# The second block's mixer reordered: memory units first, small work behind units, all 31 convolution taps on DVE

## The reference

```python
h = rms_norm(x, norm_mix_g[l]);  p = h @ w_in[l]
y_a = conformer_conv(p[:256], p[256:512], ...)   # h = a * sigmoid(g); 31-tap causal depthwise conv; layer norm; silu
y_b = head_rms_norm(moba_attention(q, k, v))      # 4 heads of 64; with 256 tokens it is one causal block
q_c, k_c, v_c = ...                               # 4 heads, 64 keys, 128 values
log_a = log_sigmoid(p_gate @ gla_gate_w + b) / 16
y_c = head_rms_norm(gla_chunked(q_c, k_c, v_c, log_a)) * silu(r)   # chunks of 32, a state of 64x128 handed on by chunk
x = x + concat([y_a, y_b, y_c]) @ w_out[l]
h = rms_norm(x, norm_ffn_g[l]);  x = x + (silu(conv3(h @ up_a)) * conv3(h @ up_g)) @ w_down
```

## Time and profile before

| | us |
|---|---|
| median of 3 runs | 2491.24 (2490.52 to 2492.51) |
| the profiled execution | 2489.02 |
| its span | 2487.2 |
| PE / DVE / ACT / POOL busy | 2311.9 / 1768.5 / 1313.8 / 194.9 |
| mean granted clock of PE | 0.944 |

### The profile page before, as it was taken

How to read it: one execution, slowest core, us unless ns; L and a number is a source line. 1 busy time by engine, 2 the same in 40 slices (tenths; PEclk the granted TensorE clock), 3 DMA queues, 4 the chain that set the end, 5 groups by cost and what they waited for, 6 DMA issues and landing times.

```text
span 2487.2 us, 42276 instructions
## 1 busy us (share of the span) xinstructions
PE 2311.9 (93%) x16453; PEld 2158.5 (87%) x16453; DVE 1768.5 (71%) x1847; ACT 1313.8 (53%) x1230; POOL 194.9 (8%) x174
## 2 busy tenths in 40 slices
PE   7998998999699999999999999996878998978998
PEld 7898997999599999999999999995858997867997
DVE  4466445456488889898888888886846776745777
ACT  4543433454277777676767776763413443422443
POOL 1000000000000000000000000003900001930000
PEclk9999998999699999999999999998859998958999
DMA  9344554535299999999999999994404545412541
GB/s 294 103 152 139 200 187 154 167 110 163 70 360 344 357 341 355 340 354 340 354 346 352 343 353 343 354 360 135 136 0 141 188 170 163 134 40 92 188 169 67
DMA packets 429633, 556.97 MB, mean 224 GB/s; under 512 B 9719, under 2 KB 385253, under 8 KB 429521
## 3 DMA queue, kind: packets, MB, share of 16 engines
q1 hardware_dynamic: 425376, 544.85, 64.8%
q0 software_dynamic: 4144, 10.64, 1.5%
HBM read 554.39 MB, written 1.06 MB: 223 GB/s over the span
## 4 chain that ended last, share of the span: by engine, by line
issue 45%; PE 40%; POOL 4%; DVE 3%; POOLq 2%; ACT 2%; DVEq 2%; DMA 1%; SPq 0%; ACTq 0%
PE ps L612 11%; PE ps L613 11%; PE ps L614 11%; POOLq L592 2%; POOL st L593 2%; POOL st L587 2%; PE ps L1220 1%; ACT w_hi L1272 1%; PE ps L1200 1%; DMA w<-in_w_in 1%; PE ps L1217 0%; PE ps L801 0%; DMA raw<-in_w_in 0%; PE ps L652 0%; DVE xn L1724 0%
## 5 line engine op out<-in xcount | busy, mean ns | idle before, releaser
L1639 DVE TENSOR_TENSOR w_lo<-raw,w_hi 128x2048 fp32r<-128x2048 f32 x519 | 1185.2, 2293 | 350.4 <-ACT w_hi L1272 347.9
L1272 ACT ACTIVATE w_hi<-raw 128x2048 fp32r<-128x2048 f32 x519 | 987.4, 1908 | 252.9 <-PE ps L614 241.8
L612 PE MATMUL ps<-w_hi,xg_hi 128*128 128x256 f32 x1792 | 512.2, 286 | 11.0 <-DVE xg_lo L2026 8.1
L612 PE MATMUL ps<-xT_hi,w_hi 128*128 128x256 f32 x1760 | 504.4, 287 | 16.2 <-DVE xT_lo L1654 8.3
L614 PE MATMUL ps<-w_hi,xg_lo 128*128 128x256 f32 x1792 | 500.6, 279 | 0.0
L613 PE MATMUL ps<-w_lo,xg_hi 128*128 128x256 f32 x1792 | 500.6, 279 | 0.0
L613 PE MATMUL ps<-xT_lo,w_hi 128*128 128x256 f32 x1760 | 499.5, 284 | 0.0
L614 PE MATMUL ps<-xT_hi,w_lo 128*128 128x256 f32 x1760 | 499.3, 284 | 0.0
L612 PEld LDWEIGHTS ps<-xT_hi,w_hi 128*128 128x128 f32 x1760 | 339.5, 193 | 23.0 <-DVE xT_lo L1654 9.1
L612 PEld LDWEIGHTS ps<-w_hi,xg_hi 128*128 128x128 f32 x1792 | 338.2, 189 | 17.7 <-issue 12.1
L613 PEld LDWEIGHTS ps<-w_lo,xg_hi 128*128 128x128 f32 x1792 | 340.2, 190 | 3.4
(11 more groups left out here) (448 smaller groups left out, 2954.3 us busy)
## 6 DMA issues: line engine op xcount, KB each, us to landing
raw<-in_exp_w SPq DMA_DIRECT2D x336, 1024.0 KB, 5.8
raw<-in_ffn_w_up SPq DMA_DIRECT2D x44, 1024.0 KB, 5.1
raw<-in_w_in SPq DMA_DIRECT2D x42, 1024.0 KB, 6.6
raw<-in_ffn_w SPq DMA_DIRECT2D x33, 1024.0 KB, 5.1
raw<-in_ffn_w_down SPq DMA_DIRECT2D x22, 1024.0 KB, 5.4
raw<-in_w_gate SPq DMA_DIRECT2D x16, 1024.0 KB, 5.3
raw<-in_w_out SPq DMA_DIRECT2D x8, 1024.0 KB, 4.9
raw<-in_w_o SPq DMA_DIRECT2D x6, 1024.0 KB, 6.1
```

The source lines that it names most:

```text
L612: pe.matmul(out, lhs[0], rhs[0], start=first, stop=False)
L1272: act.activation(w_hi[:, u.const % SPL, 0:width], raw[:, u.const % RAW, 0:width], ACT.Copy)\
L1639: dve.tensor_tensor(w_lo[:, u.const % SPL, 0:width], raw[:, u.const % RAW, 0:width], w_hi[:, u.const % SPL, 0:width].bitcast(F32), ALU.sub ...
```

## The change

The order of the units becomes: convolution (0, 1), q and k of the memory (2, 3), its values (4, 5), q, k, v of the attention (6 to 8), r (9, 10). Two PSUM banks take the projections instead of four, so a unit waits for the copy of the one two before. The small work is spread over the list of PE behind the units that give its inputs: the scores within chunks (`within_chunks`: 4 transposes and 8 matmuls) behind unit 5, all state steps behind unit 6 without waits between them, attention scores and the GLA output behind unit 7, the pairs of attention heads around and in unit 9 (`between` runs after its first half), the transposes of the results in the middle of units 10 and 11. The state steps use keys padded with zeros (`kdz`, 128 columns of which 64 are nonzero for each head, so that two heads give 128 partitions), the GLA output uses queries masked by chunk (`qgm`) and puts tokens on partitions, so its norm is a column of statistics (bn_stats) instead of matmuls with ones and a diagonal. POOL zeroes the two tiles and has no taps; DVE does all 31, in pieces of 6, 4, 3, 6, 5 and 7. The four w_out units are taken by rows (256 rows, 1024 columns) in the order 2, 1, 3, 0, so each needs a quarter of y: GLA heads 0 and 1, attention, GLA heads 2 and 3, convolution; each is 24 products of 512 columns, and the sums are closed in the last. x is then updated by quarters of 512 columns (`sums_to_x`, as after the feed-forward). The exponential subtracts the maximum by a bias on ACT instead of a pass on DVE, the gain of the attention's norm is a column of cols2, and attention and GLA outputs get their gains in the copies from PSUM. ACT's list follows the new order, with `ahead(n)` (the split of unit n+2) apart from `out(n, ...)` (wait for unit n, copy it). Before the first tap nothing moves.

The diff, cut to its core (removed lines of the old order are left out; lines with + are new, those with a blank stay):

```diff
-POOL_TAPS = range(0, 18)
-IN2_COLS = (0, 256, 512, 768, 1024, 1280, 1536, 1792, 2048, 2320, 2576)
+IN2_COLS = (0, 256, 1280, 1536, 1792, 2048, 512, 768, 1024, 2320, 2576)
+OUT2_ROWS = (2, 1, 3, 0)
+OUT2_BANKS = (1, 2, 4, 5)
...
+                pool.memset(kdz[:], 0.0)
+                pool.memset(qgm[:], 0.0).then_inc(S_.zeroed2, 1)
...
+                def state_steps():
+                    pe.wait_ge(S_.kd_ready, L + 1)
+                    pe.wait_ge(S_.at_ready, L + 1)
+                    for n in range(NCH - 1):
+                        rows = slice(GCH * (n % 4), GCH * (n % 4) + GCH)
+                        for c in range(2):
+                            for half in range(2):
+                                h = 2 * c + half
+                                m = pe.matmul(bank(4 + n % 4, 2, 2, GDV)[:, n // 4, c, :], kdz[rows, 2 * (n // 4) + c, half, :],
+                                              vc[rows, n // 4, h * GDV:(h + 1) * GDV], start=half == 0, stop=half == 1)
+                    m.then_inc(S_.ds_psum, 1)
+                def scores(tile, banks):
...
+                def gla_out():
+                    for h in range(GH):
+                        rows = slice(64 * (h % 2), 64 * (h % 2) + 64)
+                        for t in range(TT):
+                            o = ps[:, 5 + h % 2, (2 * (h // 2) + t) * P:(2 * (h // 2) + t + 1) * P]
+                            pe.matmul(o, atT[:, h, t, :], vc[:, t, h * GDV:(h + 1) * GDV], start=True, stop=False)
+                            for j in range(t == 0, 4):
+                                m = pe.matmul(o, qgm[rows, h // 2, t, j, :], st8[rows, 4 * t + j, h // 2, :],
+                                              start=False, stop=j == 3)
+                    m.then_inc(S_.o_psum, 1)
...
+                def w_out(n, chunks, between=None):
+                    pe.wait_ge(S_.yT2_lo_ready, L * 4 + n + 1)
+                    w = unit_parts(u + (11 + n), 2, D)
+                    for q, (t, h) in enumerate(QUARTERS):
+                        if between and q == 2:
+                            between()
+                        for c in range(2):
+                            m = product(ps[:, OUT2_BANKS[q], :], [v[:, t * P:(t + 1) * P] for v in chunks[c]],
+                                        [v[:, c, h * HALF:(h + 1) * HALF] for v in w], n == 0 and c == 0, n == 3 and c == 1)
+                        if n == 3 and q < 3:
+                            m.then_inc(S_.sums_closed, 1)
+                    m.then_inc(S_.unit_used, 1)
...
                 T(0, L * 8 + 24)
+                columns()
+                gate_rank()
                 T(2)
+                gate_logits()
                 T(3)
                 tok(4)
+                tok(5)
+                within_chunks()
                 T(6)
+                state_steps()
+                T(7)
+                pe.wait_ge(S_.state_ready, L + 1)
+                pe.wait_ge(S_.proj2_out, L * 11 + 8)
+                scores(0, (2, 3))
+                scores(1, (4, 7))
+                gla_out()
                 tok(8)
+                next_pair = attention(L, HB, (sb0, sb1), pT2, vb, (S_.pT2_psum, S_.pT2_ready, S_.pv2), (2, 3),
+                                      (ps[:, 4, 0:256], ps[:, 4, 256:512]))
+                pe.wait_ge(S_.proj2_out, L * 11 + 9)
...
+                pe.wait_ge(S_.proj2_out, L * 11 + 9)
+                pe.wait_ge(S_.expd2, L + 1)
+                next_pair(0)
+                tok(9, lambda: next_pair(1))
+                next_pair(2)
                 pe.wait_ge(S_.conv_ready, L + 1)
+                channel_sum(0, cvT, S_.csum_psum)
+                tok(10, lambda: gated_T(0))
+                def both_T():
+                    attended_T()
+                    pe.wait_ge(S_.yT2_lo_ready, L * 4 + 1)
+                    gated_T(1)
...
+                ahead(0)
+                ahead(1)
+                dve.wait_ge(S_.proj2_out, L * 11 + 2)
+                dve.tensor_tensor(avT[:, :, CW - 1:], avT[:, :, CW - 1:], agT[:], ALU.mult)
+                dve.drain()
+                dve.wait_ge(S_.p2_cols_ready, L + 1)
+                ahead(2)
+                convolve(6)
+                dve.wait_ge(S_.glog_psum, L + 1)
+                for c in range(2):
+                    m = dve.tensor_scalar(laT[:, c, :], ps[:, 7, c * S:(c + 1) * S], cols2[:, 68 + c:69 + c], None, ALU.add)
+                m.then_inc(S_.glog_in, 1)
+                ahead(3)
+                convolve(4)
...
+                ahead(4)
...
                 convolve(3)
...
+                dve.wait_ge(S_.gexp_ready, L * 2 + 1)
+                for c in range(2):
+                    m = dve.tensor_tensor(ends[:, c], spread(gam[:, c, :], 2, GCH), ends[:, c], ALU.subtract)
+                m.then_inc(S_.rest_ready, 1)
+                dve.wait_ge(S_.zeroed2, L + 1)
+                dve.wait_ge(S_.proj2_out, L * 11 + 4)
...
+                dve.tensor_tensor(laT[:], kcT[:], laT[:], ALU.mult)
+                dve.drain()
+                dve.tensor_tensor(qcT[:], qcT[:], egT[:], ALU.mult)
+                dve.wait_ge(S_.gexp_ready, L * 2 + 2)
+                dve.tensor_tensor(cumT[:], kcT[:], cumT[:], ALU.mult).then_inc(S_.qkg_ready, 1)
+                ahead(5)
+                convolve(6)
+                ahead(6)
+                dve.wait_ge(S_.at_psum, L + 1)
...
+                m.then_inc(S_.at_ready, 1)
+                convolve(5)
+                ahead(7)
+                dve.wait_ge(S_.ds_psum, L + 1)
...
+                        if n == 0:
+                            m = dve.tensor_copy(st8[:, 1, c, :], step)
+                        else:
+                            m = dve.scalar_tensor_tensor(st8[:, n + 1, c, :], st8[:, n, c, :], dec[:, c, n:n + 1], step,
+                                                         ALU.mult, ALU.add)
+                    if n < NCH - 2:
+                        dve.drain()
+                m.then_inc(S_.state_ready, 1)
...
+                negative_max(sb0[:], col(160, 4))
+                negative_max(sb1[:], col(164, 4))
+                ahead(8)
+                dve.wait_ge(S_.o_psum, L + 1)
+                o = [(t, h, ps[:, 5 + h % 2, (2 * (h // 2) + t) * P:(2 * (h // 2) + t + 1) * P]) for t in range(TT) for h in range(GH)]
+                var = moments([b for _, _, b in o])
+                dve.scalar_tensor_tensor(col(96, 8), var, RMS_EPS, col(104, 8), ALU.add, ALU.add).then_inc(S_.sqrt2_in, 1)
+                convolve(CW - taps[0])
+                dve.wait_ge(S_.expd2, L + 1)
+                for t, sc in enumerate((sb0, sb1)):
...
+                ahead(9)
+                dve.memset(stat[:, 0:1], 0.0).then_inc(S_.conv_ready, 1)
+                ahead(10)
...
+                gated(0)
                 dve.wait_ge(S_.pv2, L * HB + HB)
...
+                m.then_inc(S_.yb_ready, 1)
+                low(yM_lo[:, 0:2, :], 3, 70, yM_hi[:, 0:2, :], 1)
+                gated(1)
+                ahead(11)
+                low(yA_lo[:, 2:4, :], 0, 74, yA_hi[:, 2:4, :], 2)
+                low(yM_lo[:, 2:4, :], 3, 72, yM_hi[:, 2:4, :], 3)
...
+                ahead(12)
+                dve.wait_ge(S_.sqrt2_out, L * 5 + 4)
...
+                ahead(13)
+                ahead(14)
+                sums_to_x(u + 14, L * 6 + 3, None, half_square, OUT2_BANKS)
+                rms_norm(L * 5 + 5, L * 32 + 32, S_.xn_ready, 122, 2)
```

More of the change, by code:

```diff
@@ new lines, in within_chunks @@
+                def within_chunks():
+                    pe.wait_ge(S_.qkg_ready, L + 1)
+                    for t in range(TT):
+                        for c in range(2):
+                            m = pe.transpose(ps[:, 2, (2 * t + c) * P:(2 * t + c + 1) * P], kdT[:, c, t * P:(t + 1) * P], ident)
+                    m.then_inc(S_.kd_psum, 1)
+                    for h in range(GH):
+                        rows = slice(64 * (h % 2), 64 * (h % 2) + 64)
+                        for t in range(TT):
+                            m = pe.matmul(bank(3 + h % 2, 2, TT, P)[:, h // 2, t, :], kgT[rows, h // 2, t * P:(t + 1) * P],
+                                          qgT[rows, h // 2, t * P:(t + 1) * P], start=True, stop=True)
+                    m.then_inc(S_.at_psum, 1)
@@ new lines, in channel_sum @@
+                def channel_sum(col, src, done):
+                    for c in range(2):
+                        m = pe.matmul(ps[:, 7, col:col + S], ones, src[:, c, :], start=c == 0, stop=c == 1)
+                    m.then_inc(done, 1)
+                def w_out(n, chunks, between=None):
[3 more added lines that the diff above has]
+                        if between and q == 2:
+                            between()
+                        for c in range(2):
+                            m = product(ps[:, OUT2_BANKS[q], :], [v[:, t * P:(t + 1) * P] for v in chunks[c]],
[3 more added lines that the diff above has]
+                    m.then_inc(S_.unit_used, 1)
@@ L1179, in mixer2 @@
```

(45 more changed lines are left out.)

507 lines of the change are left out of this document (194 added, 313 removed).

## The result

| | before | after |
|---|---|---|
| median | 2490.88 (2490.22 to 2492.51) | 2450.19 (2449.38 to 2451.68) |
| the profiled execution | 2489.02 | 2449.39 |
| its span | 2487.2 | 2447.7 |
| mean granted clock of PE | 0.944 | 0.961 |

The ratio is 0.9836 (95% interval 0.9819 to 0.9853): 1.6% or 41 us less, clear of the noise, where 77 us were forecast, and outside the range of 2401 to 2443.

What follows compares the result with a forecast made beforehand. PE, busy 93%, was taken as the bound, losing time to waits and low clock in the second block's mixers. Saving 40.4 us less 2 for handoffs, 38.4 a layer, 77 for both: 2491.2 - 77 = 2414 us, range 2401 to 2443.

Steps and rivals of the forecast that it cites:

- (g): Mixer's tail: after the last w_lo, four quarters of 1.41 us on DVE, rms 0.9, xn at 1850.4.
- walk to xn: Layer 1's steps (a) to (g), summed without handoffs: xn at 1850.4 instead of 1890.8, 40.4 us earlier.
- (a): DVE's chain to qkg_ready ends at 1759.5, PE's units at 1755.0, so PE waits 4.5 us in within_chunks.
- rival 3: Taps keep 1.45 us instead of 0.96, their slowness not being POOL's: 13.3 us a layer, 2441; chance 0.09.
- (b): Clock falls in PE's 4.5 us gap: within_chunks takes 3.3 instead of 2.2, T(6) 5.76 + 2.9, to 1771.5.
- (c): DVE reaches at_ready at 1771.0; PE's state_steps take 6.3 us to 1777.8, T(7) runs to 1783.6.
- The tie: In (c): T(7)'s copy done at 1784.2, DVE's state steps beside it at 1784.1.
- (d): PE: scores 1.6, gla_out's 72 instructions 8.1, tok(8) 5.8, to 1799.9; DVE's conv_ready at 1808.4.
- (e): Attention pairs to first output product: conv_ready 1.9 to spare, waits of 0.8 for gated(0) and 2.7, no fall charged.
- two of its signs: T(0) to xn at a clock above 0.93; PE's next-longest mixer wait about 2.7 us, before the first output product.
- Rival 1: Clock stays low in small work and the next unit starts slow: 24 us a layer, 2462; chance 0.11.
- Rival 2: Clock falls in the wait before within_chunks and does not come back: xn 25 us later, 2542; chance 0.04.

Runs made afterwards that it cites:

- Run 3: The kernel before with only extra_sb's declaration moved behind stat, as in the change; second mixer untouched: 2514.77 us, ratio 1.0084.
- run 1: The changed kernel with extra_sb put back at the far end of the first block's scope, all tiles where they stood before: 2430.81 us, ratio 0.9744.
- Run 11: The changed kernel with useless work on POOL (120 sums of 96 columns) from the start of the second mixer: 2454.7 us, ratio 0.9851.
- Run 4: The changed kernel with DVE's convolution taps dealt out to where DVE idled, nothing else: 2430.77 us, ratio 0.9746.
- run 5: The changed kernel with extra_sb at the far place, taps dealt out to DVE's idle places, and the gated output's products grouped by row count: 2404.95 us, ratio 0.9643.
- run 10: The changed kernel with moved taps, grouped gated-output products and shifted tiles (xT, xg, yA, yM at distance 64; h2, hT at 0): 2392.74 us, ratio 0.9601.
- run 9: The changed kernel with moved taps and shifted xT and h2, plus 64 unused bytes ahead of w_hi, keeping operand distances: 2399.58 us, ratio 0.9633.

## Why the prediction was wrong

**The step that failed** is the sentence that costs what lies ahead of T(0), and the feed-forward behind, "at nothing: its instructions, loads and splits stay". They stay, but the places of their operands moved. The part ahead of T(0) took 21.4 of the 36 us between 2414 and 2450. Run 3 prices the move alone at 21 us, and run 1 brings the expert steps back to their time before; 16.4 us of the 21.4 are placed in these steps, and 4.1 lie ahead of them, which run 1 does not return. The whole diff has the moved declaration (the cut one ahead of the prediction leaves it out), and the trace of before could have warned: it had one form of product, 512 columns wide, at 0.227 (hT) and at 0.233 to 0.236 (h2), in two stretches both at full clock. No rival held this; all four were about the mixer.

The feed-forwards cost 4.3 us more, also booked at nothing. Their steps kept their pace (17.10 us before, 17.12 after), and the move has no part in it: with it alone (run 3) they take 207.6 and 205.5 us, without it (run 1) 209.4 and 207.6. The loss is at their start. PE now waits 7.5 us for xn instead of 4.2, because the four quarters of (g) stand behind the last product:

```profile
1892.38 3.51 PE L652 MATMUL ps<-cst,xn 128*128 128x128 f32 x16 [4.23 <-DVE xn L1724]
```

```profile
1880.08 3.65 PE L638 MATMUL ps<-cst,xn 128*128 128x128 f32 x16 [7.48 <-DVE xn L1756]
```

The wait itself is in the forecast's walk to xn; what it does to the clock behind it was not costed. The window behind the wait, of before and then of after, with a second fall of after some 20 us on, holds 3.4 us of low clock before and 6.0 + 3.4 after:

```profile
1892.00:1902.00 10.00, 9.62 (x69) 9.65 (x70) 4.35 (x9) 2.71 (x5) 0.61 (x1) 0.83 0.16 55
```

```profile
1880.00:1890.00 10.00, 9.92 (x61) 9.95 (x62) 4.06 (x8) 2.39 (x4) 0.55 (x1) 0.70 0.15 53
...
1906.00:1910.00 4.00, 4.00 (x23) 4.00 (x22) 3.64 (x7) 0.91 (x1) 0.00 (x0) 0.57 0.93 304
```

**The mixer.** 38.4 us a layer were forecast and 33.7 and 31.4 came, 12 short for both. For layer 1, by its steps:
- (a) DVE's chain and the wait: 4.5 forecast, 3.42 measured. Right.
- The price of a tap: 0.96 forecast, 4.71 / 5 = 0.94 measured; rival 3 is out. Run 11 shows that POOL's work did slow them, in part. By the Trainium skill, SBUF — State Buffer, section "Who interferes with whom", DVE and GpSimd share a port pair under an exclusive lock; the trace agrees in kind, ten tap instructions took 5.49 us against 4.71.
- (b) The fall was charged to within_chunks (+1.1) and T(6) (+2.9). It came, but these two took 2.3 and 7.0 us instead of 3.3 and 8.7, 2.7 less; the state steps (8.2 for 6.3) and T(7) (8.4 for 5.8) paid, 4.5 us.
- (c) PE was to reach the state steps 0.5 us after at_ready. Slowed less in T(6), it came earlier and waited 2.26: what (b) had too much and what (c) lacked nearly cancel, which is luck. The tie, T(7)'s copy against DVE's state steps, was none either: DVE was done first. Run 4 shows both waits and part of the low clock to hang on where the taps stand.
- (d) gla_out, 72 instructions at 0.112 for 8.1 us, took 11.1. This is a mis-sized term: the price was right for rows of one kind (run 5, 7.4 us), and the changes between 128 and 64 rows came on top, 3.7 us.
- (e) The 0.8 before gated(0) is 0.78; the 2.7 before the first output product was 2.1. Right. But the fall that the forecast left out there came: 12 products of the first output unit took 4.4 us instead of 3.0 (run 4), 1.4 more.
- (g) Four quarters of 1.41 behind the last w_lo: right.

The sum of these differences is -1.1 - 2.7 + 4.5 + 2.3 + 3.0 - 0.6 + 1.4 = 6.8 us. The walk to xn, without handoffs, ended at 1850.4, and xn came at 1857.1 when 21.4 is taken off: 6.7 later. The 2 us set aside for handoffs make it the 4.7 measured (146.6 - 141.9). In the main the mechanism of the forecast held in the mixer, but two of its signs failed: the clock was 0.91 and 0.92 in the windows, not above 0.93, and the wait next in length to the first was the one for at_ready. Rival 1 was right for the state steps and T(7), which ran at the low clock, and not for the rest: the clock was back at 1.00 through gla_out. Rival 2 did not occur.

## What to carry to other kernels

A new or moved declaration is an edit to every tile behind it: list where the operands of the hot products start before and after, and cost the shift like any other part of the change. Work that "stays" is only free to book if its instructions, its data's places and the clock at its start all stay. And when engines show no new wait and yet more time, compare the distance between starts of like instructions, not their durations or the busy share, which were all but the same here.

## What the runs showed of the hardware

- TensorE's fp32r products at full clock come 2 to 6% further apart according to the distance between their two operands in the partition, modulo 256 bytes: for 512 columns 0.227 us at 0 and 0.231 to 0.236 at 32, 64, 96 and 128, for 256 columns 0.113 to 0.118 at 64 and 0.120 at 0 (median of one kind, table above). What is best for one width is bad for the other (run 10: yA and yM). Moving both together by 64 bytes changes nothing (run 9). What in the chip does this is not shown. By the Trainium skill, SBUF — State Buffer, section "Who interferes with whom", PE's two read ports, for the moving operand and for the weights, are independent and only the pair that DVE shares contends. The measurements speak against full independence: the spacing depends on where the two operands stand to each other.
- Alternating products of 128 and of 64 rows costs: 11.1 us against 7.4 for the same 72 instructions, 0.20 to 0.21 us apart at and just behind a change, 0.10 to 0.12 on average among one kind (after, run 5).
- Of the low clock, 10 us remained in layer 1's mixer with waits of 0.5 and 0.9 us only ahead of it (run 4). What brings it stays open.
